# A hybrid decoder layer on one core: start of the first normalisation reordered, retention heads taken in pairs with 512-column gate projections

## What is computed

```
z = rmsnorm(x, norm_mix)
u, q, k, v, g, gate_a, gate_b = split(z @ w_in)
y_a = s5_branch(u)                       # state-space layer, GELU, GLU
y_b = retention(q, k, v) * silu(g)       # 4 heads, keys 128, values 256, chunks of 128 tokens
merged = sigmoid(gate_a) * (y_a @ P_A) + sigmoid(gate_b) * (y_b @ P_B)
h = x + merged @ w_out
h = h + relu(rmsnorm(h, norm_mlp) @ w_up)^2 @ w_down
out = rmsnorm(h, norm_final)
```

## Time and profile before

| | |
|---|---|
| median of 3 runs | 1547.88 us (1546.41 to 1547.91) |
| profiled execution, own time | 1545.83 us |
| its span | 1544.0 us |
| PE busy | 1509.7 us, 98% |
| DVE busy | 945.0 us, 61% |
| ACT, POOL busy | 301.7, 431.7 us |
| granted TensorE clock | 0.995 of full |

### The profile page before, as it was taken

One profiled execution on the slowest core, in us unless ns is written; L12 is line 12 of the kernel. 1 busy time (PEld: TensorE's weight loads), 2 busy tenths in 40 slices (PEclk: granted clock), 3 DMA queues, 4 the chain that ended last, 5 costly groups with the idle time before them and its releaser, 6 DMA issues.

```text
span 1544.0 us, 21299 instructions
## 1 busy us (share of the span) xinstructions
PE 1509.7 (98%) x7474; PEld 1264.8 (82%) x7474; DVE 945.0 (61%) x1930; ACT 301.7 (20%) x585; POOL 431.7 (28%) x363
## 2 busy tenths in 40 slices
PE   5999999999999999999999999999999999999996
PEld 4888888889898988878888888888888888888885
DVE  7896856452565646475624788665555555555557
ACT  4211111300222222231101322111111111110114
POOL 5010100421010100103333004444444444444444
PEclk9999999999999999999999999999999999999998
DMA  7124534364110110113542010111111111111113
GB/s 227 69 95 109 137 107 110 109 222 146 28 56 27 43 39 27 45 38 123 177 170 69 1 44 11 55 55 54 54 54 54 54 54 52 43 54 54 47 42 130
DMA packets 98566, 119.20 MB, mean 77 GB/s; under 512 B 16296, under 2 KB 66640, under 8 KB 98512
## 3 DMA queue, kind: packets, MB, share of 16 engines
q1 hardware_dynamic: 67520, 78.22, 16.3%
q10 hardware_dynamic: 30992, 40.26, 8.2%
HBM read 96.56 MB, written 20.97 MB: 76 GB/s over the span
## 4 chain that ended last, share of the span: by engine, by line
PE 89%; DVE 7%; ACT 2%; ACTq 1%; issue 1%; DMA 0%; DVEq 0%; SPq 0%
PE acc L648 22%; PE acc L650 22%; PE acc L649 22%; PE aux L649 6%; PE aux L648 6%; PE aux L650 6%; PE aux L912 1%; PE aux L906 1%; PE aux L915 1%; DVE zb L2083 1%; ACT h_junk L1404 1%; DVE rs_tmp L1536 1%; PE aux L800 1%; PE aux L794 0%; PE aux L901 0%
## 5 line engine op out<-in xcount | busy, mean ns | idle before, releaser
L2154 DVE TENSOR_TENSOR h_res<-h_res,acc 128x512 f32<-128x512 f32 x240 | 159.9, 685 | 98.3 <-PE acc L650 97.0
L648 PE MATMUL acc<-dw_hi,hid_hi 128*128 128x512 f32 x512 | 199.4, 390 | 0.5 <-DVE h_res L2154 0.5
L650 PE MATMUL acc<-dw_hi,hid_lo 128*128 128x512 f32 x512 | 199.2, 389 | 0.0
L649 PE MATMUL acc<-dw_lo,hid_hi 128*128 128x512 f32 x512 | 199.2, 389 | 0.0
L648 PE MATMUL acc<-w_hi,z_hi 128*128 128x256 f32 (+1 forms) x512 | 189.0, 369 | 0.0
L521 POOL CAST w_hi<-stage 128x1024 fp32r<-128x1024 f32 x44 | 49.4, 1140 | 496.0 <-PE acc L650 333.1
L648 PE MATMUL acc<-z_hi,w_hi 128*128 128x512 f32 x448 | 177.9, 397 | 3.8 <-DVE z_lo L1516 3.8
L650 PE MATMUL acc<-z_hi,w_lo 128*128 128x512 f32 x448 | 175.4, 391 | 0.0
L649 PE MATMUL acc<-z_lo,w_hi 128*128 128x512 f32 x448 | 175.3, 391 | 0.0
L650 PE MATMUL acc<-w_hi,z_lo 128*128 128x256 f32 (+1 forms) x512 | 173.0, 338 | 0.0
L649 PE MATMUL acc<-w_lo,z_hi 128*128 128x256 f32 (+1 forms) x512 | 172.8, 338 | 0.0
(11 more groups left out here) (329 smaller groups left out, 2924.4 us busy)
## 6 DMA issues: line engine op xcount, KB each, us to landing
stage<-in_w_up SPq DMA_DIRECT2D x32, 512.0 KB, 4.0
stage<-in_w_down SPq DMA_DIRECT2D x32, 512.0 KB, 3.3
stage<-in_w_in SPq DMA_DIRECT2D x28, 512.0 KB, 4.0
gate_dram<-gate_t ACTq DMA_DIRECT2D x32, 256.0 KB, 2.1
x_in<-in_x SPq DMA_DIRECT2D x8, 512.0 KB, 7.6
stage<-in_w_in SPq DMA_DIRECT2D x32, 128.0 KB, 2.5
stage<-in_w_in SPq DMA_DIRECT2D x16, 256.0 KB, 3.3
gb_t<-gate_dram ACTq DMA_DIRECT2D x16, 256.0 KB, 3.0
```

Of the source, the lines that this page charges most:

```text
L648: nc.tensor.matmul(out, s_hi, m_hi_, start=first, stop=False)
L649: nc.tensor.matmul(out, s_hi, m_lo_, start=False, stop=False)
L650: return nc.tensor.matmul(out, s_lo, m_hi_, start=False, stop=last)
L2154: V.tensor_tensor(h_res[:, c, hs], h_res[:, c, hs], acc[:, p % 4, :], ALU.add)\
```

## The change

Two parts. First, the start: the identity is loaded second, x tiles 2 and 3 before the small parameters, and the first weight load before them too. `diag` gets four buffers and is made on ACT; roots 0 and 1 are made as before one by one, roots 2 and 3 together, and those of tiles 4 to 7 as two groups of two, as single-column instructions side by side. Tiles 2 and 3 go through `acc` in place of `aux`, so PE no longer waits for DVE's `lo_z` there. The copy of `log_step` moves from DVE to ACT. Second, retention: heads by twos. One g stage covers 512 columns (two heads); a pair then runs 16 steps and three trailing ones; no hardware loop is left in this stage. The square of `o` goes to an unused part of the PSUM bank. Core of the diff:

```
-            sp.dma_start(nmix[:], ...).then_inc(const_in, 16)
-            sp.dma_start(ls_raw[...], t["log_step"]...).then_inc(ls_in, 16)
-            sp.dma_start(x_in[:, 1, :], ...)
-            sp.dma_start(ident[:], t["ident"]).then_inc(ident_in, 16)
+            sp.dma_start(ident[:], t["ident"]).then_inc(ident_in, 16)
+            sp.dma_start(nmix[:], ...).then_inc(const_in, 16)
+            sp.dma_start(x_in[:, 1, :], x_rows[:, 1, :]).then_inc(x_ready[1], 16)
+            for c in range(2, 4):
+                sp.dma_start(x_in[:, c, :], x_rows[:, c, :]).then_inc(x_ready[c], 16)
+            load(0, w_in[:, 0:2, 0:HALF])
...
# PE
-                    if n >= 4:
+                    if n >= 8:
                         pe.wait_ge(lo_done, SP_Z + n - 3)
+                    bank = acc if c in (2, 3) else aux
...
-            turn_x(0)
+            for c in range(4):
+                turn_x(c)
...
-                mm = three(acc[:, n % 4, 0:DV], z_hi[:, k, ...], z_lo[:, k, ...], wg_hi[:, k, :], wg_lo[:, k, :], ...)
+                mm = three(acc[:, n % 4, :], z_hi[:, k, ...], z_lo[:, k, ...], w_hi[:, slot, k, :], w_lo[:, slot, k, :], ...)
...
-            with pe.Fori(0, HEADS - 1) as h:
-                head(h, True)
-            head(HEADS - 1, False)
+            for p in range(N_PAIR):
+                pair(p, p < N_PAIR - 1)
...
# ACT
+            def diag_x(c):
+                act.wait_ge(x_rooted, c + 1)
+                nc.scalar.activation(diag[:, c, :], ident[:], ACT.Copy, scale=rs1[:, c:c + 1]).then_inc(diag_ready, 1)
...
# DVE
-            rstd_x(4, 4)
-            for c in range(4, NCH):
-                norm_x(c)
+            root_x(0)
+            root_x(1)
+            root_rows(2, 2, True)
+            for c in range(4):
+                lo_z(c)
+            for p in (4, 6):
+                root_rows(p, 2, False)
+                norm_x(p)
+                norm_x(p + 1)
...
+            def ret_lo(p, e, i):
+                n = LD_RET + LD_PAIR * p + 4 * e + i
+                weight_lo(n, GR_RET + 3 * p + e & 1, 2 * i, n + 1)
...
-                if n in (9, 10):
-                    weight_lo(LD_RET + n - 9, ...)
+                if n in (9, 10, 12, 13):
+                    ret_lo(0, 0, (9, 10, 12, 13).index(n))
```

More of the change, by code:

```diff
@@ L695, in turn_x @@
                     n = 2 * c + b
-                    if n >= 4:
+                    if n >= 8:
                         pe.wait_ge(lo_done, SP_Z + n - 3)
+                    if n == 11:
+                        pe.wait_ge(prm_ready, 1)
+                    bank = acc if c in (2, 3) else aux
                     for q in range(4):
                         k = 4 * b + q
-                        out, x = aux[:, n % 4, q * P:(q + 1) * P], x_in[:, c, k * P:(k + 1) * P]
+                        out, x = bank[:, n % 4, q * P:(q + 1) * P], x_in[:, c, k * P:(k + 1) * P]
                         if c < 4:
-                            mm = nc.tensor.matmul(out, x, diag[:, c % 2, :], start=True, stop=True)
+                            mm = nc.tensor.matmul(out, x, diag[:, c, :], start=True, stop=True)
                         else:
@@ L901, in score @@
                     nc.tensor.matmul(aux[:, 1, 0:P], qkt[:, 1, :], qkt[:, 0, :], start=True, stop=True)\
                       .then_inc(scores, 1)
-                    if 1 <= c < NCH - 1:
-                        pe.wait_ge(state_ready, h * (NCH - 1) + c)
-                    if c < NCH - 1:
-                        nc.tensor.matmul(aux[:, 3, 0:DV], kvk[:, c % 2, :], vv[:, c % 2, :], start=True, stop=True)
-                def attend(c):
-                    pe.wait_ge(prob_ready, cnt(c))
+                    if s % NCH < NCH - 1:
+                        if updates(s) >= 1:
+                            pe.wait_ge(state_ready, updates(s))
+                        nc.tensor.matmul(aux[:, 3, 0:DV], kvk[:, s % 2, :], vv[:, s % 2, :], start=True, stop=True)
@@ L910, in attend @@
+                def attend(s):
+                    c = s % NCH
+                    pe.wait_ge(prob_ready, cnt(s))
+                    if t0 + s >= 1:
+                        pe.wait_ge(yb_ready, cnt(s - 1))
+                    mm = nc.tensor.matmul(aux[:, 2, 0:DV], prob[:], vv[:, s % 2, :], start=True, stop=(c == 0))
                     if c >= 1:
-                        pe.wait_ge(yb_ready, cnt(c - 1))
-                    mm = nc.tensor.matmul(aux[:, 2, 0:DV], prob[:], vv[:, c % 2, :], start=True, stop=(c == 0))
@@ L1370, in _ @@
             load_ma(0)
-            with act.Fori(0, HEADS - 1) as h:
-                head(h, True)
-            head(HEADS - 1, False)
+            for p in range(N_PAIR):
+                pair(p, p < N_PAIR - 1)
             for n in range(16):
@@ L1995, in lo_early @@
                                     ALU.subtract).then_inc(yb_lo, 1)
-                for s in range(1, NCH + 2):
-                    if s <= NCH:
+                for s in range(1, STEPS_PAIR + 2):
+                    tail = s - STEPS_PAIR
+                    if tail <= 0:
                         rotate(s - 1)
-                    if s == NCH and not more:
+                    if tail == 0 and not more:
                         lo_yb(0)
@@ L2023, in head @@
                 if more:
-                    for c in range(4, NCH):
-                        g_silu(h + 1, c)
+                    for c in range(NCH):
+                        g_silu(p + 1, c)
+                        if c < 4:
+                            ret_lo(p + 1, 1, c)
                 else:
@@ L2049, in _ @@
                 if 2 <= c < 6:
-                    qkv_lo(0, c - 2)
-            with dve.Fori(0, HEADS - 1) as h:
-                ch.enter(h, PER_HEAD)
-                head(h, True)
-                ch.leave(HEADS - 1)
-            head(HEADS - 1, False)
+                    ret_lo(0, 1, c - 2)
+            for p in range(N_PAIR):
+                pair(p, p < N_PAIR - 1)
             dve.wait_ge(out_free, OUT_PB)
```

429 lines of the change are left out of this document (224 added, 205 removed).

## The result

| | before | after |
|---|---|---|
| median of 5 runs, side by side | 1546.41 us (1545.78 to 1547.91) | 1538.29 us (1537.08 to 1539.68) |
| profiled execution, own time | 1545.83 us | 1538.29 us |
| its span | 1544.0 us | 1536.5 us |
| granted TensorE clock | 0.995 | 0.996 |

The ratio after to before is 0.9946, 95% interval 0.9935 to 0.9956: faster by 0.54%, clear of noise. The forecast of 1537.6 us is met within 0.7 us, but not by its own sum: the change gives 8.1 us between the medians and 7.5 between the two profiled executions, where I had summed 10.3. The forecast also started from a median of three runs, 1547.9, that the five runs here put at 1546.4. The start was 1.5 us too high and the gain 2.2 us too large; that the two nearly cancel is luck.

The account below looks back on a forecast made before the run. PE, busy 98% of the span, was taken as the bound, so its work and waits count. g projections 5.0 plus start 5.3 make 10.3 us off 1547.9: 1537.6 us, own range 1536 to 1539, wider range 1532.0 to 1542.0.

Parts of the forecast that it names:

- The g projections: Retention's g stages: 768 matmuls of 256 columns become 384 of 512 at 0.2275 us; 5.0 us less taken.
- Rival (c): g stages: a matmul's fixed time is not saved, so they give 1.0 us, total 6.3, 1541.6 us; chance 0.03.
- The rest of the stage: Retention outside the g matmuls: fewer head ends and trailing steps, no loop, small matmuls unchanged; costed at nothing.
- The start up to the projection: Start of the kernel: the u projection begins at 22.8 us, bounds 21.6 and 24, against 26.58; gain 3.8 us.
- With x tile 1 in place at 7.74 as before: First loads: x tile 1 lands at 7.74 us, unmoved by the new order, so PE starts at 9.3, not 11.54.
- The clock: First part of the u projection: with only two waits of some 1.3 us, the clock holds; 1.7 us gained.
- Rival (b): Start gives less: clock falls once more (-1.7) or new wait is 4 us (-1.8); total 8.5, both 6.8; chance 0.17.
- The new wait: Before tile 6's transposes: PE waits 2.2 us for DVE's late `lo_z(4)`, bounds nothing and 4.
- so no: DVE's roots in the start: POOL does not hold them, as a single-column step took 0.27 us within POOL's product.
- The wait for a scaled tile: Tiles 4 and 5 in the start: tile 4 scaled at 27.4, PE comes at 28.2; no wait, 2.0 us gained.
- (d): Start hidden: DVE's chain to 126.0 does not move, PE gains only 1.4 us there; total 6.4, 1541.5 us; chance 0.03.
- Rival (e): Retention pairs: steps without a g stage between let DVE fall behind; slower from 7.82 us a step, 1553.6 at 8.0; chance 0.04.

Follow-up runs that it names:

- pairs_256: The changed kernel with each g matmul of 512 columns issued as two of 256, pairs kept: 1543.16 us, ratio 0.9978 to the kernel before.
- start_only: The kernel before with only the load order, `diag` on ACT, roots and transposes of the change: 1543.15 us, ratio 0.9979 to the kernel before.
- root_four: lo_early with one root of 128x4 for tiles 4 to 7 put back: 1539.37 us, ratio 0.9965 to the kernel before.
- pairs_only: The kernel before with only the head pairs and the rest of the retention edit: 1541.02 us, ratio 0.9968 to the kernel before.
- lo_before: The kernel before with `lo_z(4)` right behind the scaling of tile 5 and `lo_z(5)` behind tile 7: 1546.63 us, ratio 1.0005 to the kernel before.
- lo_early: The changed kernel with `lo_z(4)` right behind the scaling of tile 5 and `lo_z(5)` behind tile 7: 1534.24 us, ratio 0.9920 to the kernel before.
- lo_early_2: The same kernel as lo_early, run again in another set on another chip: 1534.74 us, ratio 0.9928 to the kernel before.

## Why the prediction was right, and where it failed

**The g projections: right.** 0.2269 us for a matmul of 512 columns where 0.227 was taken, 5.0 us for the width by two ways (43.56 against twice 23.03, and pairs_256). By the rule of the Trainium skill (TensorE: Matmul & The Clock Gate, "Wait — 56ns, not 53.3ns?") two matmuls made one would save some 2.5 ns, an estimate from the page's fixed cost; the rows give 2 x 0.120 - 0.227 = 0.013 us, five times as much, and the measurement decides. Rival (c), built on that rule, is out. "The rest of the stage ... I cost both at nothing" was wrong by 0.5 us, of which the joins of heads inside the pairs cost 0.4.

**The start up to the projection: right in its steps, 0.6 us short.** "With x tile 1 in place at 7.74 as before" failed: it was there at 8.62, and PE began at 10.21 rather than 9.3. Most of that lateness is the identity, which now goes ahead of it: loaded fourth, it left the tile at 7.98 to 8.15. `diag` on ACT took 0.39 us where 0.35 was taken. The gain was 3.2, not 3.8.

**The clock: the step that failed.** "It stands some 1.3 us twice. I say it holds": it did hold there, but I did not ask the same of the wait that I had myself put before tile 6. A wait of 2.6 us, as long as the 2.66 us behind which the clock fell before, had the same fall behind it. The 1.7 us were counted as gained and were only moved. Of the 2.8 us that the sum lacked, this is the largest part. Rival (b) had its price, "the clock falls once more (-1.7)", and its total of 8.5 is nearest to the 8.1 between the medians, but it placed it at the two short waits near the projection. In these traces each of the waits of 2.6 to 2.9 us that stood within the projection or right ahead of it has such a fall behind it (before, the change, start_only, pairs_256, root_four, pairs_only); the waits of 1.8 us and less in the change and its variants have none. In between the traces disagree: the 2.0 us of lo_before, ahead of a tile, had the long fall behind it, while the 2.0 us and 1.9 us for the scaled tile, before and in pairs_only, had none (the clock is 1.00 over 35 to 41 us in both). So the length of one wait does not tell it all. No edit took away the wait without the fall or the fall without the wait, so that the wait is the cause is argued from these, not shown by itself.

**The new wait: right, with two errors that met.** It was forecast at 2.2 us, with PE there at 38.1 and the first half of `lo_z(4)` done at 40.3. PE was there at 39.19, that half was begun at 40.99 and done at 41.7, and the wait was 2.64: DVE was 1.4 us late and PE 1.1, and the two nearly cancel. Inside, tiles 4 and 5 were to be scaled by 28.7 and were at 31.7, held by POOL; the next two were put behind POOL and ran free of it, 34.97 to 37.45, done 1.4 us later than the forecast 36.1. The GPSIMD Engine Reference of the Trainium skill (table of specifications) names DVE instructions with two SBUF inputs: these traces agree, 5.13 against 2.48 us. Its other half, by which the prediction said that a root step could be held too, did not show in the single-column roots; but the one-input steps of four columns in lo_before were held, 0.89 and 2.23 us instead of 0.16 and 0.17. So the prediction's "so no" holds for single-column steps alone. In which mode DVE ran those steps, no trace here shows.

**The wait for a scaled tile, and DVE's chain: right.** The 2.0 us are gone, and root_four shows that the roots two by two did it. The start is not hidden, which rules out (d): DVE had the first batch's state at 123.6 instead of 126.0, and PE used it at 124.96 instead of 127.42, without a wait and with the same 1.4 us of room. In lo_early that room is down to 0.4 us, and in lo_early_2 PE waits 0.37 us there. A wait that the prediction left out stands at the second batch: 1.3 us for `hst` before, 0.7 in the change.

**The sum.** Start 5.3 forecast, 3.0 measured: -0.6 at the projection's start, -1.7 for the clock, -0.4 for the longer wait, +0.6 for `hst` at the second batch, and some 0.2 that I did not trace. Retention 5.0 forecast, 4.5 measured. Rival (e) is out: no step of retention shows a wait of PE beyond the 1.1 us that stood there before.

## What to carry to other kernels

When an edit brings work forward, look for the operation that now comes late, and price it twice where it stops a busy TensorE: the wait and the stretch at half clock that may follow it. Here moving `lo_z(4)` and `lo_z(5)` ahead of work that PE does not yet wait for was worth 3 to 4 us, beside the 8 that the whole change brought. And fuse narrow float32 matmuls that share a stationary operand: here each matmul less saved 13 ns.

## What was not expected of the hardware

- Where DVE's scalings and POOL ran together, both got longer, as if they took turns: two scalings took 5.13 us instead of 2.48, POOL's subtraction 3.25 instead of 2.37, and its second cast 2.04 instead of 1.04, while the cast that had begun first kept its 1.04.
- POOL also held DVE steps of 128x4 with a single tensor input (2.23 us instead of 0.17 in lo_before), but not steps of 128x1 (0.46 us for two, with and without POOL).
- The clock's fall took the same 3.4 us at the lower level in six kernels, and 10.1 us in one execution of lo_before, whose projection started 2.4 us late; PE had made that up by the first C tile.
- Moving one load of 64 KB (the identity, 128x128) ahead of two others moved the start of x tile 1's square from about 8.0 us (three executions) to between 8.6 and 10.3 (eight executions).
